# Dense blocks transpose the raw residual and scale the products; the other blocks transpose a normalized tile

## The reference

```python
for l in range(2):
    hdn = swiglu(rms_norm(x, norm_pre[l, 0]), ...)      # blocks 0 and 3, "ffn"
    x = x + 0.5 * rms_norm(hdn, norm_post[l, 0])
    h = rms_norm(x, norm_pre[l, 1])
    mix = ...                                           # block 1 attention + recurrence, block 4 convolution
    x = x + rms_norm(mix, norm_post[l, 1])
    hdn = swiglu(rms_norm(x, norm_pre[l, 2]), ...)      # blocks 2 and 5, "ffn"
    x = x + 0.5 * rms_norm(hdn, norm_post[l, 2])
# rms_norm(x, g) = x * rsqrt(mean(x*x) + 1e-6) * g
# swiglu(h, wg, wu, wd) = (silu(h @ wg) * (h @ wu)) @ wd, inner width 2816
```

## Time and profile before

| | us |
|---|---|
| median of 3 runs | 2751.63 (2750.99 to 2753.77) |
| span of the profiled execution | 2747.2 |
| TensorE busy | 2600.3 (95%) |
| VectorE busy | 2165.5 (79%) |
| ScalarE busy | 1483.6 (54%) |
| GpSimd busy | 947.8 (34%) |

### The profile page before, as it was taken

One profiled execution on the slowest core, in us unless ns is written; L12 is line 12 of the kernel. 1 busy time (PEld: TensorE's weight loads), 2 busy tenths in 40 slices (PEclk: granted clock), 3 DMA queues, 4 the chain that ended last, 5 costly groups with the idle time before them and its releaser, 6 DMA issues. The chain is left out here.

```text
span 2747.2 us, 47482 instructions
## 1 busy us (share of the span) xinstructions
PE 2600.3 (95%) x17802; PEld 2379.0 (87%) x17802; DVE 2165.5 (79%) x2488; ACT 1483.6 (54%) x1930; POOL 947.8 (34%) x586
## 2 busy tenths in 40 slices
PE   8999899999998998888998978999999999999997
PEld 7999699999897998658998747999999999999986
DVE  5667666766787676987855997898989898989888
ACT  4337543443434334424334515777777777777765
POOL 6990089688789992126900130000000000000000
PEclk9999999999999998999999988999999999999999
DMA  8664267566566653324553415999999999999985
GB/s 309 252 237 148 103 241 256 202 250 254 191 241 229 220 183 134 115 105 164 183 184 138 164 63 192 343 350 333 352 335 349 338 347 343 347 345 346 340 320 216
DMA packets 129209, 670.58 MB, mean 244 GB/s; under 512 B 14672, under 2 KB 14992, under 8 KB 80064
## 3 DMA queue, kind: packets, MB, share of 16 engines
q1 hardware_dynamic: 111024, 604.72, 59.9%
q0 software_dynamic: 18064, 64.21, 6.9%
HBM read 667.82 MB, written 1.05 MB: 243 GB/s over the span
## 5 line engine op out<-in xcount | busy, mean ns | idle before, releaser
L1721 PE MATMUL work<-xT_hi,wh_gu 128*128 128x256 f32 x2088 | 593.9, 284 | 21.6 <-DVE xT_lo L985 12.0
L1722 PE MATMUL work<-xT_lo,wh_gu 128*128 128x256 f32 x2088 | 592.3, 284 | 0.0
L1723 PE MATMUL work<-xT_hi,wl_gu 128*128 128x256 f32 x2088 | 591.7, 283 | 0.0
L1721 PE MATMUL work<-wh_gu,mixT_hi 128*128 128x256 f32 x1792 | 507.5, 283 | 2.8 <-DVE wl_gu L1439 1.5
L1722 PE MATMUL work<-wl_gu,mixT_hi 128*128 128x256 f32 x1792 | 505.8, 282 | 0.0
L1723 PE MATMUL work<-wh_gu,mixT_lo 128*128 128x256 f32 x1792 | 505.5, 282 | 0.0
L857 DVE TENSOR_TENSOR wl_gu<-raw_gu,wh_gu 128x2048 fp32r<-128x2048 f32 x158 | 392.3, 2483 | 72.0 <-ACT wh_gu L395 71.5
L1721 PEld LDWEIGHTS work<-xT_hi,wh_gu 128*128 128x128 f32 x2088 | 401.3, 192 | 30.1 <-issue 21.3
L1722 PEld LDWEIGHTS work<-xT_lo,wh_gu 128*128 128x128 f32 x2088 | 401.7, 192 | 4.8
L1723 PEld LDWEIGHTS work<-xT_hi,wl_gu 128*128 128x128 f32 x2088 | 401.5, 192 | 0.0
L862 DVE TENSOR_TENSOR wl_d<-raw_d,wh_d 128x1024 fp32r<-128x1024 f32 x157 | 250.2, 1594 | 189.6 <-ACT wh_d L402 189.5
(11 more groups left out here) (436 smaller groups left out, 4785.6 us busy)
## 6 DMA issues: line engine op xcount, KB each, us to landing
raw_gu<-in_w_gu SPq DMA_DIRECT2D x271, 1024.0 KB, 5.2
raw_d<-in_w_d SPq DMA_DIRECT2D x269, 512.0 KB, 5.4
scratch<-in_w_gu SPq DMA_DIRECT2D x112, 1024.0 KB, 7.2
scratch<-in_w_d SPq DMA_DIRECT2D x112, 512.0 KB, 7.8
scratch<-in_w_mod POOLq DMA_DIRECT2D x96, 512.0 KB, 3.7
scratch<-in_s_b POOLq DMA_DIRECT2D x16, 256.0 KB, 2.9
rows<-in_norm_post POOLq DMA_DIRECT2D x6, 512.0 KB, 4.4
rows<-in_ln_g POOLq DMA_DIRECT2D x4, 512.0 KB, 5.5
```

The costliest lines, as they stand in the source:

```text
L1721: pe.matmul(out_, w[0], m[0], start=start, stop=False)
L1722: pe.matmul(out_, w[0], m[1], start=False, stop=False)
L1723: return pe.matmul(out_, w[1], m[0], start=False, stop=stop)
```

## The change

In the four dense blocks of the first model (0, 2, 3 and 5, `RAW_FFN`) TensorE transposes X as it stands, as soon as `x_first` and `x_done` are signalled. The 256 token scales are applied to the products: ScalarE sums the squares of t = 0 ahead of the `XH` pieces and those of t = 1 behind `XH` and `hi_gu(n0 + 1)`, then takes both roots and loads the Silu table. VectorE inverts them (`token_scales`), TensorE spreads them into a row on all partitions with two fp32 matmuls between the first and the second `gate_up` (`scale_row`), and VectorE copies that row to SBUF (`RS_ROW`). In every step VectorE multiplies the gate half by the row, ScalarE takes SiLU of that, and VectorE multiplies the up half by the row and then the two together: three multiplies where there was one.

Blocks 1 and 4 write the normalized tile `XN` (128 by 1024 per token half) in the place of the diagonal, and TensorE transposes it. `mod_columns` moves ahead of the last `down` in block 2. Counts of the semaphore `xn_done` follow. VectorE's and ScalarE's loops have their first two steps written out.

```diff
-                    for t in range(NT):
+                    def own_squares(t):
...
                         squares(t, X[:, t, :])
-                        root(eps_rms, t)
-                    if SUBS[b][0] == "ffn":
-                        load_table(ACT.Silu)
+                    own_squares(0)
+                    if b not in RAW_FFN:
+                        root(eps_rms, 0)
+                        own_squares(1)
+                        root(eps_rms, 1)
                     if b == 0:
                         act.wait_ge(cols_in, 16)
                         hi_gu(0)
...
+                    if b in RAW_FFN:
+                        hi_gu(START[b] + 1)
+                        own_squares(1)
+                        for t in range(NT):
+                            root(eps_rms, t)
+                        load_table(ACT.Silu)
                     if b == 0:
                         act.activation(c_act, C("c", 0, KD), ACT.Silu).then_inc(c_act_done, 1)
                         hi_d(0)
...
+                        if b in RAW_FFN:
+                            ge(act, gate_scaled, SCALED[b] + n - n0 + 1, at)
+                            act.activation(SG[n % 2], SG[n % 2], ACT.Silu).then_inc(silu_done, 1)
...
-                    for t in range(NT):
-                        rstd(t)
-                        TS(RS_DIAG[t], ident, rs[:, t:t + 1], None, ALU.mult).then_inc(xn_done, 1)
+                    if b not in RAW_FFN:
+                        for t in range(NT):
+                            rstd(t)
+                            TS(XN[:, t, :], X[:, t, :], rs[:, t:t + 1], None, ALU.mult).then_inc(xn_done, 1)
...
+            def token_scales():
+                for t in range(NT):
+                    roots[0] += 1
+                    dve.wait_ge(root_done, roots[0])
+                    dve.reciprocal(rs[:, t:t + 1], rs[:, t:t + 1]).then_inc(rs_ready, 1)
+                scale_rows[0] += 1
+                dve.wait_ge(rs_ps, scale_rows[0])
+                link(dve.tensor_copy(RS_ROW, PB[:, 3, 0:S]))
...
                     lo_gu(n + 1, j)
+                    if first:
+                        token_scales()
+                    if raw:
+                        ge(dve, gu_used, n + 1, j)
+                        TT(SG[k], PB[:, k, 0:S], RS_ROW, ALU.mult).then_inc(gate_scaled, 1)
+                        link(TT(HF[k], PB[:, k, S:2 * S], RS_ROW, ALU.mult))
+                        dve.wait_ge(silu_done, j + (f0 + r + 1))
+                        link(TT(HF[k], SG[k], HF[k], ALU.mult))
...
-                        if b < SECOND:
-                            last = pe.matmul(turned(t, k), X[:, t, cols_k], RS_DIAG[t], start=True, stop=True)
-                        else:
-                            last = pe.transpose(turned(t, k), src[:, t, cols_k], ident)
+                        last = pe.transpose(turned(t, k), src[:, t, cols_k], ident)
...
+            def scale_row():
+                scale_rows[0] += 1
+                pe.wait_ge(rs_ready, NT * scale_rows[0])
+                for t in range(NT):
+                    last = pe.matmul(PB[:, 3, t * P:(t + 1) * P], rs[:, t:t + 1].broadcast_to([P, P]), ident,
+                                     start=True, stop=True)
+                last.then_inc(rs_ps, 1)
...
                 gate_up(n0, dyn)
+                if n0 < START[SECOND]:
+                    scale_row()
                 gate_up(n0 + 1, dyn)
...
-                if n0 == MOD_START[3]:
-                    mod_columns(3)
+                if n0 in (MOD_START[1], MOD_START[3]):
+                    mod_columns(MOD_START.index(n0))
...
                 down(n0 + nf - 1, dyn, f0 + nf - 1, fdyn, False, True)
-                if n0 in MOD_START[0:3]:
+                if n0 in (MOD_START[0], MOD_START[2]):
                     mod_columns(MOD_START.index(n0))
```

81 lines of the change are left out of this document (47 added, 34 removed).

## The result

The changed kernel took 2778.45 us (median of 4 runs, 2773.25 to 2780.74) beside 2751.31 us for the kernel before (4 runs on the same chip). The ratio is 1.0088, with a 95% interval of 1.0068 to 1.0108. Measured again later, beside other kernels, it was 1.0088 once more (1.0070 to 1.0106). So the change costs about 24 us by the ratio (0.0088 of 2751; the plain difference of these two medians is 27). The forecast was +4.4 us with 2765 as its upper end. "Slower" was its second likeliest outcome, and the size was wrong by a factor of five.

What follows compares the result with a forecast made beforehand. It took TensorE to bound the steps, so only the start and block boundaries could move: +8.4 - 1.8 - 1.65 + 4.1 - 1.4 - 3.25 = +4.4 us, giving 2756.0 us, range 2748 to 2765.

Steps and rivals of the forecast that it cites:

- "Slower": Outcome for the whole kernel: a measured time above the kernel before by more than about 0.2%; chance 0.40.
- Inside the steps: 0 us: In the 88 dense steps, two more VectorE operations each cost nothing, h coming 1.3 us later against 5 us cover.
- block 4's -1.4: Boundary into block 4: the normalized tile with transposes saves 1.8 us, less 0.4 for the clock, giving -1.4 us.
- rival C: Dense steps lengthen as GpSimd's terms collide with VectorE's new multiply; 0.1 us in 84 steps gives +8.4, 2764.4; chance 0.11.
- The start, +8.4: Start of block 0: second gate_up waits behind squares, roots, table loads and weight rounding, ending at 38.4 instead of 30.0.
- GpSimd starts no later: Ahead of block 1: block 0's later steps move back 8 us while GpSimd does not, so its delay of lo_d goes.
- The moved columns, +2.0 of block 3's +4.1: End of block 2: columns ahead of the last down lose their cover and slow that down; gate start +2.0 us.
- GpSimd's sums were ready in time there: End of block 2: the moved mod_columns would not have to wait for GpSimd's modulation sums; no charge of its own.
- The lower clock at gate start: Gate starts behind idle time run at lower clock: +1.6 us at blocks 2, 3, 5; 0.5 at blocks 1, 4.
- rival A: Transposes leave the lower clock at gate starts of blocks 1 and 4 too: +1.1 and +1.2, total 2758.3; chance 0.19.
- Blocks 2 and 5, -3.75 and -5.35 at the gate: Boundaries into blocks 2 and 5: transposing unscaled X starts the gate 3.75 and 5.35 us earlier, before clock and scale_row charges.

Runs made afterwards that it cites:

- experiment 3: GpSimd's modulation multiply-adds replaced by memsets in both the changed kernel and the kernel before; ratios 1.0001 and 0.9960 to the kernel before.
- Experiment 11: Kernel before plus one unread VectorE product of two 128x256 SBUF tiles in each dense step of blocks 0, 2, 3 and 5; ratio 1.0065.
- experiment 1: Changed kernel with block 0's first down weights rounded ahead of the second gate weights, squares and roots; ratio 1.0076 to the kernel before.
- Experiment 9: Changed kernel with SiLU written to PSUM in raw dense steps and the up product ahead of the gate product; ratio 1.0116 to the kernel before.
- experiment 2: Changed kernel with block 2's one-column modulation products put back behind its last down product; ratio 1.0051 to the kernel before.
- experiment 10: Kernel before with only block 2's one-column modulation products moved ahead of its last down product; ratio 1.0028.
- experiment 6: Changed kernel with block 0 as before, columns moved back, and identity products filling TensorE's idle time between transposes of blocks 2 and 5; ratio 1.0017.
- experiment 7: Changed kernel with the diagonal product again in blocks 1 and 4, 4 alone, or 1 alone; ratios 1.0047, 1.0060 and 1.0077 to the kernel before.
- e4_after_no_sums: Changed kernel with GpSimd's modulation multiply-adds left out and memsets in their place; ratio 1.0001 to the kernel before.
- e18_before_extra: Kernel before plus one unread VectorE product of two SBUF tiles in each dense step of blocks 0, 2, 3 and 5; ratio 1.0065.

## Why the prediction was wrong, step by step

Two steps of the prediction failed most: "Inside the steps: 0 us", and block 4's -1.4.

**Inside the steps: 0 us.** From the fourth `gate_up` on the steps did stay 8.53 us apart, and rival C as it was put did not come. But this term was put at nothing on a cover of 5 us read from a step in the middle of a block, and it failed in two ways. First, in the first steps of blocks 2 and 3 the cover was not there: VectorE's operations were stretched beside GpSimd's terms, `down(0)` waited 1.42 and 1.31 us for h, and the third `gate_up` came 2.4 us later than without the sums (experiment 3), in each of the two blocks. Second, I asked whether the added VectorE work would delay TensorE, and not whom else it delays: GpSimd's terms, which run beside these steps, and for whose sum TensorE waits at the end of blocks 0, 2 and 3. Experiment 11 gives the price of that on the kernel before, +18 us for one product a step. In after it is the other half of a tie, with waits of 0.13, 0.60 and 0.00 us, and what it adds there to TensorE's own delay isn't measured by itself; it is why repairing TensorE's side alone brings nothing (experiment 1). Experiment 3 takes both ways together, and block 4 below: 13 of the 24 us go when the sums go. The first sign stood in the trace of before, where `mod_columns` of blocks 0 and 3 waited 0.6 us for GpSimd. What in VectorE's work lengthens the terms is open. Experiment 9 gives no sign that it is one product's operands, and it is not the amount alone: with two more operations a step the terms of after took 184 to 186 us, with one more in experiment 11 187 to 188.

**The start, +8.4.** Measured +7.5 on TensorE (third `gate_up` at 40.15 in place of 32.65), by the mechanism given: `hi_d(0)` at 24.88 behind the roots, the second `gate_up` at 30.04, the lower clock behind it. The gap ahead of it was 3.15 us and not 6, since the first `gate_up` itself ran at the lower clock up to about 23.3; that cost nothing, as the second had to wait anyway. What failed is the sentence under block 1 that "GpSimd starts no later". The SiLU of c, which GpSimd waits for, moved from 17.09 to 24.78 behind the roots, and the first term from 24.48 to 29.17. The sum so ended 7.5 us later, and experiment 1 shows that repairing TensorE's side alone brings nothing.

**The moved columns, +2.0 of block 3's +4.1.** Sign right, size wrong. In after they cost 10 us (experiment 2), on the kernel before 7.7 (experiment 10). I had the half-clock `down` and the lost cover. I missed that "GpSimd's sums were ready in time there" held for the one execution profiled, in which the terms took 174.8 us; in blocks 0 and 3 of the same trace, and in block 2 of experiment 10's, they took 183. In experiment 10's trace the wait was 3.65 us and the columns behind it took 10.40, as long as in the window at half clock of experiment 11.

**The lower clock at gate start.** Right in kind and too small at two places: I charged 0.5 at blocks 1 and 4 and 1.6 elsewhere, and all five fell to about 0.65, some 2 us each. That is rival A, and by its own sum it would explain 2.3 us of the 20 that are missing. The Trainium skill's rule (TensorE: Matmul & The Clock Gate, "Part 4: PE-mode transpose"), by which transposes don't count as work for the clock, agrees with these five windows. It also agrees with experiment 6, where ordinary products set between the transposes brought 1.00 back. That such a block always starts low, as the prediction drew from it, is not what the runs show: in all traces together 55 gate starts stand behind transposes without filler, and 11 of them had the full clock, among them block 3 of experiment 2 and block 1 in the second trace of after. In blocks 2 and 5 it was low every time.

**Block 4, -1.4.** Wrong in sign: about 8 us come back with the diagonal there, 11 with block 1's as well (experiment 7). In the traces the stretch behind this gate is the largest single part of the miss, +4.8 us where -4.95 was forecast, and it shrinks from 118.8 to 106.3 without the sums (in the kernel before from 114.1 to 109.4). So the price is VectorE's work in block 4 falling on GpSimd's terms. That the slow beginning behind the transposes is what brings this about in most executions is an association (experiment 7) and not shown. I had looked at this boundary up to the gate start and not at the 110 us behind it.

**Blocks 2 and 5, -3.75 and -5.35 at the gate.** Right, in mechanism and size. From the end of the last product of the block before to the gate start are 8.05 us in place of 11.72 at block 2 (-3.67), and 9.88 in place of 15.17 at block 5 (-5.29). Over the kernels with the diagonal in block 4, block 4 to 5 took 109.9 us on average (five traces with block 5 raw) and 114.5 (three with it as before, their sums in place), 4.6 us less. Some 2 us of it are given back by the clock (experiment 6), and part in the first step, where h was late.

## What to carry to other kernels

Before adding work to an engine that has time to spare, look for every chain that ends in a wait, not only the one that bounds the steps; a wait of 0.6 us at a block's end can mean that two chains tie, and here what brought the hidden one's end 5.7 us later (212.74 in place of 207.01, block 0 of experiment 11) made that wait 5.88 us. Undoing a delay on one side of a tie shows nothing (experiment 1), so test both sides, or take the second chain away altogether (experiment 3). And where a stretch is timed from one profiled execution, ask for a second trace before a margin is called slack: GpSimd's row of terms took 175 or 183 us with the same code.

## What the runs showed of the hardware that was not expected

Where GpSimd's terms run, VectorE's operations on SBUF tiles are at times stretched and those fed from PSUM are not. Block 2's first step in the kernel after, where TensorE then waited 1.42 us for h:

```profile
362.35 0.42 DVE L1109 TENSOR_TENSOR scratch<-work,scratch 128x256 f32<-128x256 f32 x1
362.69 0.42 DVE L1110 TENSOR_TENSOR scratch<-work,scratch 128x256 f32<-128x256 f32 x1
363.32 1.37 DVE L1112 TENSOR_TENSOR scratch<-scratch 128x256 f32<-128x256 f32 x1 [0.22 <-ACT scratch L544]
364.73 1.56 DVE L1116 CAST h_hi<-scratch 128x256 fp32r<-128x256 f32 x1
366.32 2.55 DVE L1117 TENSOR_TENSOR h_lo<-scratch,h_hi 128x256 fp32r<-128x256 f32 x1
```

The two that read PSUM keep their 0.42 us; h_lo takes 2.55 in place of the 0.43 of the earlier trace rows. The last two end at 366.29 and 368.87, just behind the ends of the two operations that GpSimd had beside them (366.14 and 368.59). Over blocks 2 and 3 of that trace the PSUM-fed products of 128x256 took 0.40 to 0.42 us without exception, and the three operations on SBUF tiles up to 1.73, 1.56 and 2.60; in the same blocks without the sums (e4_after_no_sums) none of the three took more than 0.43.

The one-column products of a sum (48 of 128x1) took 5.6 to 9.2 us when TensorE came to them from work or after a wait of at most 2.4 us. They took 10.4 in all seven cases with a wait of 5.9 to 6.0 ahead, and 9.4 and 10.4 in the two with 3.6; where a window was taken, over the first such case of e18_before_extra, the granted clock was 0.50 all through. In these cases an idle time of some 6 us thus cost itself and some 3 us more in the narrow products behind it.
